# State-space stage: the imaginary input sum of the scan moves from VectorE to GpSimd

## The chip, the cores and the metric

The kernel runs on one core of a Trainium2 chip. The metric is the device time of one execution in microseconds; the time before is the median of three executions. TensorE is called PE, VectorE DVE, ScalarE ACT, GpSimd Pool, and SyncE SP. SP here only issues DMAs.

## The reference, cut to what matters

One decoder layer is applied to 2048 prompt positions and to 64 sample positions: an RMS norm, a diagonal complex state-space mixer (S5), a residual sum, a second norm, a top-2 mixture of 16 experts, and a final norm. The change touches the recurrence of the mixer alone:

```python
lb_re = mag * jnp.cos(ang)
lb_im = mag * jnp.sin(ang)
...
_, _, st_re, st_im = lax.associative_scan(
    _linear_recurrence_combine, (a_re, a_im, bu_re, bu_im), axis=1)
y = (jnp.einsum('gcp,bsgp->bsgc', c_re.astype(f32), st_re)
     - jnp.einsum('gcp,bsgp->bsgc', c_im.astype(f32), st_im)
     + d.astype(f32) * u)
y = jax.nn.gelu(y.reshape(nb, ns, SSM_WIDTH)).astype(x.dtype)
a = y @ w_out
```

There are 32 groups of 64 complex states. The state follows s[k] = lambda * s[k-1] + b[k] with complex lambda. The kernel turns the input back by the angle of lambda to the power k, so that what is left is a real recurrence with the magnitude alone, on the real and on the imaginary part separately; it scans both, and turns the result forward again.

## The kernel before, in words

The kernel has three stages on PE. Stage A projects x to u (until 118 us). Stage B is the state-space stage (118 to 190 us). Stage C is the output projection, gate, norm and router (190 to some 440 us), and after it come the expert matmuls, bound by PE, until the end.

Stage B works in `PR` = 16 rounds r, each for two of the 32 groups, on 128 partitions (2 groups x 64 states) by 256 chunks of 8 positions. `turns(r)` gives the cosine and sine tables of the round in `WT`. For each round:

- PE `b_state(r)` (L1196): eight matmuls write the real and imaginary inputs into two PSUM banks (`v_done`).
- DVE `b_rot(r)` (L1767, L1768): `r1` = v x cosine and `r2` = v x sine, both 128x512 (real and imaginary half), v in PSUM and the table in SBUF (`rot_done`). `r1` has two buffers, `r2` has one.
- DVE `b_mix(r)`: `z[:,0]` = r1 real + r2 imaginary (L1782) and `z[:,1]` = r1 imaginary - r2 real (L1785), 128x256 each, all of it in SBUF (`z_done`). `z` has one buffer for both halves.
- DVE `b_scan(r)` (L1775): the scan of the real and then of the imaginary half, into `r1` (`scan_done`).
- DVE `b_turn(r)` (L1793, L1794): scan result x cosine into `Sc`, x sine into `Ss`, 128x512 each, SBUF only (`turned_on`).
- PE `b_out(r)` (L1214, L1219): the direct term from the table `T`, and the states times C, into PSUM (`y_done`). ACT `b_gelu(r)` (L823) writes the result over `U` (`gelu_done`). Pool `b_final(r)` (L524, L525) takes the last state of the round out of `Sc` and `Ss`: two instructions on one column.

DVE issues them in the order rot(r+1), scan(r), mix(r+1), turn(r). Every engine runs its own list in order; semaphores tie them.

The table `T` is filled in four parts n of eight groups each. Pool clears a part (L515 for the first, L529 for the other three, at the head of its rounds 0, 1 and 2) and signals `t_zero`. SP waits for it (L349) and issues eight DMAs from `Kp` into the part (L352); `b_out` waits for a part at rounds 0, 4, 8 and 12. Behind the 32 DMAs of `T`, SP's list goes on with the 4 MB load of `w_out` (L356), the load of the last gain (L358), and then, three times, a store of eight groups of y to DRAM (`y_by_block`, L362, after 8, 16 and 24 GELUs), a wait until it has landed (L363), and eight loads that bring it back in another layout (L365). Stores and loads of the last eight groups follow (L372, L377). Stage C begins on PE with `c_half` (L1259), which waits for all 24 loads of L365 (`y_in`).

Two memsets at Pool's start (L471, L472) have the semaphore `c_pool`, for which ACT (L780) and PE (L1167) wait; ten index tables that Pool makes behind stage B have `consts`, for which DVE waits (L1913).

Of the kernel before, what the change touches and what calls it, by code (L numbers as in the profile page):

```python
# [9 lines left out]
ALU = mybir.AluOpType  # L10
# [14 lines left out]
PR = G // 2  # L25
# [7 lines left out]
EPS = 1e-6  # L33
# [38 lines left out]
def hybrid_kernel(nc, x_rows, x_first, x_cols, s0, par, bc_in, d_in, gmix, gffn, gfin, w_in, w_out, w_route,  # L72
# [9 lines left out]
    with outer:  # L82
        scope = [outer]

        def sb(name, shape, dt=F32):
            return scope[0].enter_context(nc.sbuf_tensor(name, shape, dt))

        def sem(name):
            return outer.enter_context(nc.semaphore(name))
# [8 lines left out]
        ones = sb("ones", [P, P])  # L98
# [38 lines left out]
        epsc = sb("epsc", [P, 1])  # L137
# [23 lines left out]
        r1 = [sb(f"r1{b}", [P, 2, NP_CH]) for b in range(2)]  # L161
        r2 = sb("r2", [P, 2, NP_CH])
        z = sb("z", [P, 2, NP_CH])
# [29 lines left out]
        for n in (0, 1):  # L193
# [65 lines left out]
        wst.close()  # L259


        names = """par_in gm_in bc_in win0 win1 win2 win3 win4 win5 win6 win7 rt_in gl_in dch act_small c_g1 c_pool 
            x_in0 x_in1 xrow_in0 xrow_in1 w1_hi w1_lo xh_done xl_done sq_done std_done rin_done um_done us_done us8_in tr_done ue_act ue_dve
            kd_ready f0_ready ph_ready pws_ready pool_chain cl_ready e_ready wt_small tabs_ready k_done k_evac k_full et_done et_evac
            t_zero t_in0 t_in1 t_in2 t_in3 v_done rot_done z_done scan_done turned_on sp_zero sp_head cl_neg fo_done y_done gelu_done
            y_stored yt_st0 yt_st1 yt_st2 yt_st3 y_in y_tail fo_raw fo_sum st_stored
            wout_in w2_hi w2_lo ys_hi ys_lo a_done sig_done x2_done xr_in0 xr_in1 x2_st0 x2_st1 wr_scaled xt_done xt_evac lt_done lt_evac fold_set rl_done rl_evac ssq_done half_ss dchc
            dchd exp_d consts tab_set tab_clear d_ready pos_done pos_read idx_done tab_early tab_in tab_first tab_ready tot_done words_set words_done ctl_done exp_in rec_set
# [2 lines left out]
        S = {n: sem(n) for n in names}  # L271
# [193 lines left out]
        def _(pool):  # L465
# [2 lines left out]
            ch(pool.affine_select(out=ident[:, :], in_=ident[:, :], compare_op=ALU.not_equal, fill=1.0, base=0,  # L468
                                  pattern=[[-1, P]], channel_multiplier=1))
            ch(pool.memset(power[:, :], -0.5))  # L470
            pool.memset(epsc[:, :], EPS).then_inc(S["c_pool"], 1)  # L471
            pool.memset(ones[:, :], 1.0).then_inc(S["c_pool"], 1)  # L472
            ch(pool.memset(upper[:, :], 1.0))

            ch(pool.affine_select(out=upper[:, :], in_=upper[:, :], compare_op=ALU.is_gt, fill=0.0, base=0,
# [44 lines left out]
            def b_final(r):  # L520

                b = r % SB
                pool.wait_ge(S["turned_on"], 2 * r + 2)
                pool.tensor_tensor(FO[:, 0, r, DECB:DECB + 1], Sc[b][:, 0, NCH:NCH + 1], Ss[b][:, 1, NCH:NCH + 1], ALU.subtract).then_inc(S["fo_done"], 1)  # L524
                pool.tensor_tensor(FO[:, 1, r, DECB:DECB + 1], Sc[b][:, 1, NCH:NCH + 1], Ss[b][:, 0, NCH:NCH + 1], ALU.add).then_inc(S["fo_done"], 1)  # L525

            for r in range(PR):
                if r < 3:
                    pool.memset(T[:, 8 * r + 8:8 * r + 16, :], 0.0).then_inc(S["t_zero"], 1)  # L529
                b_final(r)  # L530
# [175 lines left out]
        def _(act):  # L706
# [70 lines left out]
            act.wait_ge(S["c_g1"], 1)  # L777
            act.activation(AN[:, 3, :, :], AN[:, 1, :, :], ACT.Sin).then_inc(S["act_small"], 1)
            act.activation(AN[:, 4, :, :], AN[:, 2, :, :], ACT.Sin).then_inc(S["act_small"], 1)
            act.wait_ge(S["c_pool"], 2)  # L780
            for t in range(1, TA):
                if t < TA - 1:
                    x_hi(t + 1)
# [305 lines left out]
        def _(pe):  # L1089
            def a_first():  # L1090

                pe.wait_ge(S["xl_done"], 1)
                for k in range(KD):
                    pe.wait_ge(S[f"win{k}"], 16)
                    for h in range(2):
                        mm = pe.matmul(pbig[h * ST:(h + 1) * ST, 0, 0:W // 2], x0g[:, k, :], w1[:, k, h * W // 2:(h + 1) * W // 2],
                                       start=(k == 0), stop=(k == KD - 1))
                mm.then_inc(S["um_done"], 1)
# [65 lines left out]
                        mm = pe.transpose(bank[:, (2 * a + r) * P:(2 * a + r + 1) * P], E[:, a, 2 * f + r, :], ident[:, :])  # L1164
                mm.then_inc(S["et_done"], 1)

            pe.wait_ge(S["c_pool"], 2)  # L1167
            a_first()
            for t in range(1, TA):
                a_tile(t)  # L1170
# [386 lines left out]
        def _(dve):  # L1557
            ch = Chain(dve, S["dch"])
            tt, ts, stt = dve.tensor_tensor, dve.tensor_scalar, dve.scalar_tensor_tensor
# [197 lines left out]
            def turns(r):  # L1757
                return [WT[:, a:a + 1, r, :].to_broadcast([P, 2, NP_CH]) for a in range(2)]

            def b_rot(r):  # L1760

                b = r % 2
                v = pbig[:, 2 * b:2 * b + 2, DECB:NCH]
                dve.wait_ge(S["v_done"], r + 1)
                if r >= 1:
                    dve.wait_ge(S["z_done"], 2 * r)
                tt(r1[b][:, :, :], v, turns(r)[0], ALU.mult).then_inc(S["rot_done"], 1)  # L1767
                tt(r2[:, :, :], v, turns(r)[1], ALU.mult).then_inc(S["rot_done"], 1)  # L1768

            def b_scan(r):  # L1770
                b = r % 2
                dve.wait_ge(S["z_done"], 2 * r + 2)
                mg = mag8[:, r:r + 1].to_broadcast([P, NP_CH])
                for a in range(2):
                    dve.tensor_tensor_scan(r1[b][:, a, :], mg, z[:, a, :], 0.0, ALU.mult, ALU.add).then_inc(S["scan_done"], 1)  # L1775

            def b_mix(r):
                b = r % 2
                dve.wait_ge(S["rot_done"], 2 * r + 2)
                if r >= 1:  # L1780
                    dve.wait_ge(S["scan_done"], 2 * r - 1)
                tt(z[:, 0, :], r1[b][:, 0, :], r2[:, 1, :], ALU.add).then_inc(S["z_done"], 1)  # L1782
                if r >= 1:
                    dve.wait_ge(S["scan_done"], 2 * r)
                tt(z[:, 1, :], r1[b][:, 1, :], r2[:, 0, :], ALU.subtract).then_inc(S["z_done"], 1)  # L1785

            def b_turn(r):
                b, q = r % 2, r % SB
# [5 lines left out]
                tt(Ss[q][:, :, DECB + 1:NCH + 1], r1[b][:, :, :], turns(r)[1], ALU.mult).then_inc(S["turned_on"], 1)  # L1794

            b_rot(0)
            b_mix(0)
            for r in range(PR):
                if r + 1 < PR:
                    if r >= 1:  # L1800
                        dve.wait_ge(S["turned_on"], 2 * r)
                    b_rot(r + 1)
                b_scan(r)
                if r + 1 < PR:
                    b_mix(r + 1)
                b_turn(r)
# [103 lines left out]
                    yy = y_  # L1910

            dch = Chain(dve, S["dchd"])
            dve.wait_ge(S["consts"], 10)  # L1913
            dch(dve.memset(logit[LAST:P, 0, :], 0.0))
            dch(dve.memset(EP[:, 0, :], 0.0))
            dch(dve.memset(te[:, 0, :], 1.0))
# [358 lines left out]
```

## Time and profile before

| | us |
|---|---|
| median of three executions | 825.34 (823.92 to 826.82) |
| profiled execution, whole | 825.51 |
| its span | 823.8 |
| PE busy in the span | 786.2 (95%) |
| DVE busy | 598.0 (73%) |
| ACT busy | 412.6 (50%) |
| Pool busy | 321.7 (39%) |

All times in the text are microseconds from the start of the span. The profiled execution lies 0.17 us above the median and 1.7 us above its own span. The granted clock is a share of 2.4 GHz: 1.00 is that, 0.50 is 1.2 GHz. In a timeline, instructions of one kind that follow each other may stand in one row with a count.

### The profile page before, as it was taken

The page shows a single profiled execution, that of the slowest core. Times are in us where ns is not written, and L with a number is a line of the kernel's source. Part 1 is how long each engine was busy: PE and PEld are TensorE (multiplying, and loading weights), DVE is VectorE, ACT ScalarE, POOL GpSimd, SP SyncE. Part 2 cuts the span into 40 slices and gives each one's busy share as a digit, 9 for nine tenths or more (in the row PEclk, how much of TensorE's full clock was granted, in tenths as well). Part 3 has the DMA queues.
Part 4 walks back from the last instruction along what each step waited for, and adds up shares of the span by engine and source line. Part 5 has one row for each costly group of instructions (what it writes and reads, how often), then busy time and mean ns, then how long its engine had stood idle before and what let it go on. Part 6 is the DMA issues. An engine that isn't in the chain of part 4 may idle for free.

```text
span 823.8 us, 15189 instructions
## 1 busy us (share of the span) xinstructions
PE 786.2 (95%) x4265; PEld 620.0 (75%) x4265; DVE 598.0 (73%) x1143; ACT 412.6 (50%) x770; POOL 321.7 (39%) x416
## 2 busy tenths in 40 slices
PE   6999989999999999999989989999999999999993
PEld 4888866655778787877767878888888888888772
DVE  7997789996533374556876788768687688687843
ACT  7556752124334543333353666657466576466631
POOL 3920011002000001322455576667666766566533
PEclk9999999999999999999999999999999999999997
DMA  8564315989742433424357587658775688786632
GB/s 304 162 225 180 129 25 162 234 165 204 289 154 90 141 121 110 154 78 155 104 214 284 207 306 271 212 180 263 272 256 199 207 291 299 249 301 196 236 121 81
DMA packets 57671, 161.27 MB, mean 196 GB/s; under 512 B 21857, under 2 KB 26465, under 8 KB 50913
## 3 DMA queue, kind: packets, MB, share of 16 engines
q1 hardware_dynamic: 34304, 112.99, 42.0%
q0 software_dynamic: 22976, 47.05, 16.4%
q8 instruction: 44, 0.72, 0.3%
q14 instruction: 59, 0.48, 0.2%
q10 hardware_dynamic: 288, 0.03, 0.0%
HBM read 129.07 MB, written 62.40 MB: 232 GB/s over the span
## 4 chain that ended last, share of the span: by engine, by line
PE 42%; DVE 3%; issue 3%; DVEq 1%; ACT 1%; ACTq 0%; POOL 0%; POOLq 0%
PE pbig L1395 8%; PE pbig L1399 8%; PE pbig L1396 8%; PE pbig L1414 4%; PE pbig L1416 4%; PE pbig L1415 4%; PE pbig L1331 4%; PE pbig L1407 1%; DVE WL L2018 0%; ACT WH L932 0%; DVEq L2128 0%; DVE hh L1863 0%; PE pbig L1352 0%; DVEq L2126 0%; PE pbig L1358 0%
## 5 line engine op out<-in xcount | busy, mean ns | idle before, releaser
L1395 PE MATMUL pbig<-WH,xgH 128*128 (+1 forms) x304 | 123.0, 404 | 1.2 <-issue 1.1
L1396 PE MATMUL pbig<-WL,xgH 128*128 (+1 forms) x304 | 119.0, 391 | 0.0
L553 POOL DMA_INDIRECT records<-rec,at_rec x34 | 38.8, 1140 | 191.2 <-DVEq L2011 158.9
L1278 PE MATMUL pbig<-w2H,ysH 128*128 128x512 f32 x256 | 105.3, 411 | 0.0
L1279 PE MATMUL pbig<-w2L,ysH 128*128 128x512 f32 x256 | 100.6, 393 | 0.0
L1280 PE MATMUL pbig<-w2H,ysL 128*128 128x512 f32 x256 | 100.5, 393 | 0.0
L2018 DVE SCALAR_TENSOR_TENSOR WL<-WR,gf_p,WH 128x512 f32 (+1 forms) x128 | 86.2, 746 | 0.0
L932 ACT ACTIVATE WH<-WR,gf_p 128x512 f32 (+1 forms) x128 | 80.8, 713 | 3.0 <-DMA WR<-in_w_gu 0.9
L1399 PE MATMUL pbig<-WH,xgL 128*128 (+1 forms) x304 | 77.0, 395 | 0.0
L627 POOL DMA_INDIRECT x_sums<-xg,recs x36 | 60.7, 1685 | 35.4 <-DVE xg L2122 21.5
L2122 DVE SCALAR_TENSOR_TENSOR xg<-pbig,recs,xg 128x1024 f32<-128x1024 f32 x39 | 49.9, 1280 | 27.8 <-PE pbig L1416 27.8
L950 ACT ACTIVATE sl<-pbig,recs 128x256 f32<-128x256 f32 x40 | 19.0, 475 | 98.0 <-PE pbig L1399 92.6
L1395 PEld LDWEIGHTS pbig<-WH,xgH 128*128 128x128 f32 x304 | 57.1, 188 | 14.4 <-issue 2.5
L1399 PEld LDWEIGHTS pbig<-WH,xgL 128*128 128x128 f32 x304 | 57.0, 188 | 13.7
L1414 PE MATMUL pbig<-WH,hTH 128*128 (+1 forms) x160 | 66.4, 415 | 0.0
L1396 PEld LDWEIGHTS pbig<-WL,xgH 128*128 128x128 f32 x304 | 57.1, 188 | 11.3
L1890 DVE TENSOR_TENSOR x<-pbig,sg 128x1024 f32<-128x1024 f32 x16 | 19.6, 1223 | 62.8 <-PE pbig L1280 58.3
L1416 PE MATMUL pbig<-WH,hTL 128*128 (+1 forms) x160 | 63.3, 396 | 0.0
L1415 PE MATMUL pbig<-WL,hTH 128*128 (+1 forms) x160 | 62.5, 390 | 0.0
L1278 PEld LDWEIGHTS pbig<-w2H,ysH 128*128 128x128 f32 x256 | 48.2, 188 | 13.8 <-issue 4.6
L1863 DVE SCALAR_TENSOR_TENSOR hh<-pbig,recs,sl 128x256 f32<-128x256 f32 x40 | 19.3, 483 | 53.4 <-issue 28.8
L655 POOL DMA_INDIRECT out_y<-fo,recs x40 | 49.6, 1240 | 19.2 <-issue 9.9
(356 smaller groups left out, 1745.9 us busy)
## 6 DMA issues: line engine op xcount, KB each, us to landing
WR<-in_w_gu SPq DMA_DIRECT2D x32, 1024.0 KB
WR<-in_w_dn SPq DMA_DIRECT2D x16, 1024.0 KB
xT<-in_x_cols SPq DMA_DIRECT2D x16, 512.0 KB, 3.6
low<-in_x_rows SPq DMA_DIRECT2D x16, 512.0 KB, 4.3
U<-in_x_rows SPq DMA_DIRECT2D x16, 512.0 KB, 5.4
x_mid<-x SPq DMA_DIRECT2D x16, 512.0 KB
x_sums<-x SPq DMA_DIRECT2D x16, 512.0 KB
w<-in_w_out SPq DMA_DIRECT2D x1, 4096.0 KB, 13.7
```

Of the source, the lines that this page charges most:

```text
L627: pool.indirect_dma_start(sumD, bass.IndirectOffsetOnAxis(ap=recs_u[:, t, SUM_AT:SUM_AT + 1], axis=0), xg[t % RING][:, :], None, bounds_ch ...
L932: act.activation(WH[:, ds(to + k * 2 * DE, 2 * DE)], WR[:, k * 2 * DE:(k + 1) * 2 * DE], ACT.Copy, scale=gf_p[:, k:k + 1]).then_inc(S["hi_ ...
L1278: pe.matmul(pbig[:, n, :], ysH[b][:, k, :], w2H[n][:, k, :], start=(k == 0), stop=False)
L1279: pe.matmul(pbig[:, n, :], ysH[b][:, k, :], w2L[n][:, k, :], start=False, stop=False)
L1280: mm = pe.matmul(pbig[:, n, :], ysL[b][:, k, :], w2H[n][:, k, :], start=False, stop=(k == CB - 1))
L1395: pe.matmul(pbig[:, 6, :], xgH[b][:, k, :], WH[:, ds(off + k * 2 * DE, 2 * DE)], start=(k == 0), stop=False)
L1396: pe.matmul(pbig[:, 6, :], xgH[b][:, k, :], WL[:, ds(low_ + k * 2 * DE, 2 * DE)], start=False, stop=False)
L1399: mm = pe.matmul(pbig[:, 6, :], xgL[b][:, k, :], WH[:, ds(off + k * 2 * DE, 2 * DE)], start=False, stop=(k == KD - 1))
L1414: pe.matmul(out, hTH[b][:, k, :], WH[:, w], start=(k == 0), stop=False)
L1415: pe.matmul(out, hTH[b][:, k, :], WL[:, ds(low_ + at, 512)], start=False, stop=False)
L1416: mm = pe.matmul(out, hTL[b][:, k, :], WH[:, w], start=False, stop=(k == 1))
L2018: stt(WL[:, ds(low_ + w, 2 * DE)], WR[:, w:w + 2 * DE], gf_p[:, k:k + 1], WH[:, ds(to + w, 2 * DE)].bitcast(F32), ALU.mult, ALU.subtract). ...
```

## The change

The instruction L1785 leaves `b_mix` on DVE. Pool gets a function `b_mix_im(r)`, which computes the same subtraction after `rot_done` of round r and after both scans of round r-1. Pool issues it for round 0 ahead of its round loop, and for round r+1 at the head of iteration r, ahead of the memset of `T` and of `b_final(r)`. It signals a new semaphore `z_im`. On DVE, `b_rot(r)` waits for `z_done` r and for `z_im` r; `b_scan` waits for `z_done` ahead of the real scan and for `z_im` ahead of the imaginary one. The semaphore `c_pool` is merged into `consts`, whose last wait becomes 12.

```diff
-            pool.memset(epsc[:, :], EPS).then_inc(S["c_pool"], 1)
-            pool.memset(ones[:, :], 1.0).then_inc(S["c_pool"], 1)
+            pool.memset(epsc[:, :], EPS).then_inc(S["consts"], 1)
+            pool.memset(ones[:, :], 1.0).then_inc(S["consts"], 1)
...
+            def b_mix_im(r):
+
+                b = r % 2
+                pool.wait_ge(S["rot_done"], 2 * r + 2)
+                if r >= 1:
+                    pool.wait_ge(S["scan_done"], 2 * r)
+                pool.tensor_tensor(z[:, 1, :], r1[b][:, 1, :], r2[:, 0, :], ALU.subtract).then_inc(S["z_im"], 1)
+
+            b_mix_im(0)
             for r in range(PR):
+                if r + 1 < PR:
+                    b_mix_im(r + 1)
                 if r < 3:
                     pool.memset(T[:, 8 * r + 8:8 * r + 16, :], 0.0).then_inc(S["t_zero"], 1)
                 b_final(r)
...
                 if r >= 1:
-                    dve.wait_ge(S["z_done"], 2 * r)
+                    dve.wait_ge(S["z_done"], r)
+                    dve.wait_ge(S["z_im"], r)
                 tt(r1[b][:, :, :], v, turns(r)[0], ALU.mult).then_inc(S["rot_done"], 1)
                 tt(r2[:, :, :], v, turns(r)[1], ALU.mult).then_inc(S["rot_done"], 1)

             def b_scan(r):
                 b = r % 2
-                dve.wait_ge(S["z_done"], 2 * r + 2)
                 mg = mag8[:, r:r + 1].to_broadcast([P, NP_CH])
                 for a in range(2):
+                    dve.wait_ge(S["z_im" if a else "z_done"], r + 1)
                     dve.tensor_tensor_scan(r1[b][:, a, :], mg, z[:, a, :], 0.0, ALU.mult, ALU.add).then_inc(S["scan_done"], 1)
...
                 tt(z[:, 0, :], r1[b][:, 0, :], r2[:, 1, :], ALU.add).then_inc(S["z_done"], 1)
-                if r >= 1:
-                    dve.wait_ge(S["scan_done"], 2 * r)
-                tt(z[:, 1, :], r1[b][:, 1, :], r2[:, 0, :], ALU.subtract).then_inc(S["z_done"], 1)
...
-            dve.wait_ge(S["consts"], 10)
+            dve.wait_ge(S["consts"], 2 + 10)
```

The waits of ACT and PE for `c_pool` 2 become waits for `consts` 2.

## Rows read from the trace of the kernel before

**Rows 1.** Timeline of PE, stage B (start, us, engine, line, operation, [idle before <- releaser]).
```profile
126.23 1.11 PE L1196 MATMUL pbig<-U,E 128*64 128x264 f32 x8
...
130.34 1.11 PE L1196 MATMUL pbig<-U,E 128*64 128x264 f32 x8
...
188.97 0.61 PE L1219 MATMUL pbig<-turned_s,CLn 64*128 64x264 f32 x4
190.63 5.37 PE L1259 MATMUL pbig<-w,U 128*64 128x512 f32 x24 [1.05 <-DMA U<-y_by_block]
```

**Rows 2.** Timeline of SP's DMA queue, stage B (when SP issued; not the landing).
```profile
114.84 21.52 SPq L352 DMA_DIRECT2D T<-Kp  x32
136.40 0.59 SPq L356 DMA_DIRECT2D w<-in_w_out  x1
...
139.36 0.33 SPq L362 DMA_DIRECT2D y_by_block<-U  x1
154.38 3.65 SPq L365 DMA_DIRECT2D U<-y_by_block  x8
158.07 0.43 SPq L362 DMA_DIRECT2D y_by_block<-U  x1
167.08 3.62 SPq L365 DMA_DIRECT2D U<-y_by_block  x8
174.16 0.34 SPq L362 DMA_DIRECT2D y_by_block<-U  x1
180.01 3.62 SPq L365 DMA_DIRECT2D U<-y_by_block  x8
```

**Rows 3.** Windows: each engine's busy time, then granted clock, DMA share, GB/s.
```profile
168.00:176.00 8.00, 7.65 (x52) 4.63 (x50) 7.97 (x16) 1.71 (x8) 0.33 (x2) 1.00 1.13 143
```

**Rows 4.** Timeline of DVE: one large product, the head of stage B, and round 0.
```profile
111.49 1.22 DVE L1709 TENSOR_TENSOR WT<-WT,tabs 128x1024 f32<-128x1024 f32 x1
...
118.80 0.43 DVE L1782 TENSOR_TENSOR z<-r 128x256 f32<-128x256 f32 x1
...
119.66 0.69 DVE L1767 TENSOR_TENSOR r<-pbig,WT 128x512 f32<-128x512 f32 x1
...
120.87 1.26 DVE L1775 TENSOR_TENSOR_SCAN r<-sm,z 128x256 f32<-128x256 f32 x2
122.05 0.40 DVE L1782 TENSOR_TENSOR z<-r 128x256 f32<-128x256 f32 x1
122.36 0.42 DVE L1785 TENSOR_TENSOR z<-r 128x256 f32<-128x256 f32 x1
122.70 0.69 DVE L1793 TENSOR_TENSOR turned_c<-r,WT 128x512 f32<-128x512 f32 x1
...
124.02 0.69 DVE L1767 TENSOR_TENSOR r<-pbig,WT 128x512 f32<-128x512 f32 x1
```

**Rows 5.** Timeline of Pool: a 256-element product, a memset, a one-element sum.
```profile
35.94 1.62 POOL L488 TENSOR_TENSOR low<-WT,tabs 128x256 f32<-128x256 f32 x1
...
114.92 0.95 POOL L529 MEMSET T<- 128x1024 f32 x1
...
185.09 0.51 POOL L524 TENSOR_TENSOR FO<-turned_c,turned_s 128x1 f32<-128x1 f32 x1 [4.03 <-DVE turned_s L1794]
```

**Rows 6.** Timeline of DVE beside the Pool product of rows 5.
```profile
35.26 1.82 DVE L1668 TENSOR_TENSOR p<-tabs 128x1152 f32<-128x1152 f32 x1
37.00 1.77 DVE L1669 TENSOR_TENSOR CL<-tabs 128x1152 f32<-128x1152 f32 x1
38.81 1.66 DVE L1670 TENSOR_TENSOR CL<-p,CL 128x1152 f32<-128x1152 f32 x1
```

**Rows 7.** Windows as in rows 3: early in stage A, and behind PE's last matmul.
```profile
50.00:52.00 2.00, 2.00 (x7) 1.54 (x6) 1.97 (x2) 0.63 (x3) 0.00 (x0) 0.50 0.91 356
...
810.00:811.00 1.00, 0.39 (x2) 0.00 (x0) 0.57 (x1) 0.81 (x3) 0.70 (x2) 1.00 0.44 176
...
813.00:814.00 1.00, 0.00 (x0) 0.00 (x0) 0.59 (x1) 0.00 (x0) 0.81 (x2) 0.66 0.00 0
```

More of the change, by code:

```diff
@@ L259, in hybrid_kernel @@
         wst.close()
-        names = """par_in gm_in bc_in win0 win1 win2 win3 win4 win5 win6 win7 rt_in gl_in dch act_small c_g1 c_pool
+        names = """par_in gm_in bc_in win0 win1 win2 win3 win4 win5 win6 win7 rt_in gl_in dch act_small c_g1
             x_in0 x_in1 xrow_in0 xrow_in1 w1_hi w1_lo xh_done xl_done sq_done std_done rin_done um_done us_done us8_in tr_done ue_act ue_dve
             kd_ready f0_ready ph_ready pws_ready pool_chain cl_ready e_ready wt_small tabs_ready k_done k_evac k_full et_done et_evac
-            t_zero t_in0 t_in1 t_in2 t_in3 v_done rot_done z_done scan_done turned_on sp_zero sp_head cl_neg fo_done y_done gelu_done
+            t_zero t_in0 t_in1 t_in2 t_in3 v_done rot_done z_done z_im scan_done turned_on sp_zero sp_head cl_neg fo_done y_done gelu_done
             y_stored yt_st0 yt_st1 yt_st2 yt_st3 y_in y_tail fo_raw fo_sum st_stored
@@ L779, in _ @@
             act.activation(AN[:, 4, :, :], AN[:, 2, :, :], ACT.Sin).then_inc(S["act_small"], 1)
-            act.wait_ge(S["c_pool"], 2)
+            act.wait_ge(S["consts"], 2)
             for t in range(1, TA):
@@ L1165, in e_spread @@
                 mm.then_inc(S["et_done"], 1)
-            pe.wait_ge(S["c_pool"], 2)
+            pe.wait_ge(S["consts"], 2)
             a_first()
```

## The prediction

> **What bounds the kernel now.** The page says that PE is busy for 95% of the span, so time is lost or won where PE waits. I read PE's timeline first, around the edited stage. In stage B a round of PE, from one `b_state` to the next, takes 4.11 us while nothing holds it [rows 1]: its own work. DVE's timeline has no idle time in stage B; its round takes 4.36 us, from L1767 at 119.66 to L1767 at 124.02 [rows 4], so DVE paces the stage from about round 5 on and shortening its list looks like a gain. But PE's last matmul of stage B ends at 189.58 (188.97 + 0.61), and the first matmul of stage C starts at 190.63, with 1.05 us idle put down to the DMA that brings y back [rows 1]. What releases stage C is not DVE's last round. It is the chain on SP's queue.
>
> So the third view is SP's timeline [rows 2]. Thirty-two DMAs of `T` are issued in one run from 114.84, then `w_out` at 136.40, the first store of y at 139.36. SP's next instruction, the loads, starts at 154.38, when that store has landed. Loads, store 2 at 158.07, landed at 167.08; loads, store 3 at 174.16, landed at 180.01; loads, and 190.63 is 10.6 behind them. Is that chain bound by the GELUs or by the transfers? Store 2 was issued right behind its loads and landed 12.70 after store 1. Store 3 was issued 3.39 later than it could have been (174.16 against 170.77, which is 167.08 + the 3.69 that SP needed the time before), since it waited for 24 GELUs; it landed 12.93 after store 2. **Issuing it 3.39 us late cost 0.23.** The transfers bound the chain: the loads in small pieces keep the DMA engines full (share 1.13) from 168 to 176 at only 143 GB/s [rows 3], and the store queues behind them.
>
> Two consequences. A faster DVE gives at most 0.23 us back. And whatever delays the landing of store 1 reaches stage C nearly in full.
>
> **The change part by part.**
>
> *Semaphore `c_pool` merged into `consts`*: the same number of signals and waits. The first two signals still come first, as Pool's list has them at its start. Nothing.
>
> *L1785 leaves DVE.* Its slot is 122.36 to 122.70 [rows 4], so 0.34 a round is saved.
>
> *Pool makes the difference while DVE works.* The Pool instruction for round r+1 may start when both scans of round r are done. Behind them DVE has L1782, L1793 and L1794, all with two inputs from SBUF. How the two engines go beside each other is in the early part of the trace: Pool's 256-element product takes 1.62 (35.94 to 37.56) [rows 5] while DVE's product of 1152 elements ends at 37.08 (35.26 + 1.82) [rows 6]. Pool is done 0.48 after DVE's instruction ends; it has waited for it. DVE pays too: alone a 1024-element product takes 1.22 and a 256-element one 0.40 [rows 4], which is 0.82 for 768 elements, so 1152 elements take 1.22 + 128 x 0.82/768 = 1.36 alone, but the three took 1.82, 1.77 and 1.66 [rows 6]: 0.46, 0.41 and 0.30 more, in the mean 0.39. The scan does it as well: the one-element sum of Pool that lay beside a scan took 0.51 [rows 5]. So the handover works at the ends of instructions, and I price it at 0.39 on DVE for each Pool instruction, with 0.30 and 0.46 as ends. The net on a round is 0.39 - 0.34 = +0.05, between -0.04 and +0.12.
>
> The Trainium skill, page "SBUF — State Buffer", section "Who interferes with whom", says that a VectorE instruction with two SBUF inputs and a GpSimd instruction that reads SBUF exclude each other, and that whoever starts first holds the port for the whole instruction. The waiting in rows 5 and 6 agrees. By the page "GPSIMD Engine Reference" a two-input operation needs at least some 2.5 cycles per element, an estimated 0.53 us here; by both rules DVE would lose 0.53 a round, +0.19 net, which would leave my sum as it is, since the sum doesn't go by the round.
>
> *New waits on DVE.* `b_rot(r+2)` now waits for Pool's result. Pool is ready at L1782's end + 0.48. In round 0 that is 122.45 + 0.48 = 122.93, against 124.02 for L1767: 1.1 us of cover. If Pool lost each handover until L1794 had ended, it would be done 0.48 behind it, and a round would be 0.48 + 0.07 - 0.34 = +0.19 to +0.25 longer. The wait ahead of the second scan is met long before. At the very start there is no cover: L1782 ends at 119.23, Pool at 119.71, and with 0.07 of handing on (an estimate from the gap between dependent Pool instructions such as L488 and the next) the second L1767 starts at 119.78 instead of 119.66: +0.12, once. Over 16 rounds DVE is late by 0.12 + 16 x 0.05 = 0.9 us (-0.5 to +2.0). PE's stage B then ends at 190.5.
>
> *The memset of `T` moves behind two of the new instructions.* This is the step that decides. Before, Pool cleared part 1 at 114.92, long before SP wanted it [rows 5]. Now that memset stands behind `b_mix_im(0)` and `b_mix_im(1)`, and the latter needs both scans of round 0. These end at 120.87 + 1.26 = 122.13, plus 0.12: 122.25. L1782 then holds Pool until 122.57, Pool ends at 123.05, the memset (0.95) at 124.0, SP sees it at 124.1. SP wants it after its first eight DMAs: 114.84 + 8 x 21.52/32 = 120.22 [rows 2]. **SP stands still for 3.9 us.** Ends: 3.4 if Pool's instruction took some 0.2 and never waited, 4.6 if it also waited for L1793. The memsets of parts 2 and 3 come at some 128.4 and 132.8 and SP wants them at 129.5 and 134.9: no more loss. No `b_out` suffers: round 1 needs its part at 126.23 + 1.04 [rows 1], so round 4 needs part 1 three PE rounds later, at 139.6, and its last DMA is issued by 129.5.
>
> Behind the `T` DMAs everything on SP is 3.9 later: `w_out` at 140.3. Store 1 waits behind it, at 141.4 instead of 139.36. It landed 18.0 us behind the issue of `w_out` (136.40 to 154.38) [rows 2], with 4 MB ahead of it on the same queue. I take that distance as fixed: store 1 lands at 158.3, +3.9. Bounds: +2.0 if only its own issue counted, +4.6 with the worst memset. Store 2 lands at 158.3 + 12.70 = 171.0, SP is free for store 3 at 174.7; its GELUs are ready at 174.16 + 0.12 + 12 x 0.05 = 174.9. As 3.4 us of lateness cost 0.2, this 0.2 costs nothing, and it lands 12.7 to 12.9 later, at 183.7. Against 180.01 that is +3.7: the 3.9 less the 0.2 that the idle time gives back. Only if the round of DVE grew by more than 0.3 (3.7 over 12 rounds) would the GELUs come last.
>
> *Stage C* starts at 190.63 + 3.7 = 194.3. ACT makes its first copy of y, the last GELUs and the weight copies behind the same loads, and the last stores and loads follow in SP's list, so all of these move with it. Behind 190.63 PE is nearly always busy and the rest hangs on it; I see nothing that would take the 3.7 back.
>
> **Sum.** 825.51 + 3.7 = 829.2 for an execution like the profiled one, which was 0.17 above the median; against 825.34 it is 829.0, +0.45%.
>
> **Rivals.**
>
> *A. The transfers take the delay back, and it is not slower.* Store 1 may not have been bound by the bytes of `w_out` but by its own issue; then it lands 2.0 later, store 3 1.8 later, and the time is 827.1, within 0.3%. For it: the DMA engines were not full in every slice between 136 and 154. Against it: 15 us for 1 MB where store 3 took 5.9. It decides from a landing of store 1 before 157.1 (+2.7) on. 15%.
>
> *B. PE's clock falls in the longer gap.* PE would stand still from 190.5 to 194.3. Behind its last matmul, which ends inside 810 to 811, the granted clock is down to 0.66 in 813 to 814 [rows 7]; this gap would be as long. Elsewhere the clock stood at 0.50 (1.2 GHz) for a whole stretch of 2 us [rows 7]; 2 to 3.4 us like that at the head of stage C would cost 1.0 to 1.7: 830.5. Against it: the gap may be a little too short. 11%.
>
> *C. The port costs more than the early rows say, and DVE's round becomes the bound.* From +0.3 a round on each further 0.1 costs 1.6 us at the end of stage B; +0.5 gives 197.6 for PE's end, +7: 832.4. Against it: three rows with at most 0.46 of loss, and even when Pool loses all handovers the round grows by only 0.25. 6%.
>
> *D. The gain that the edit seems to promise.* With a free port DVE's round would be 4.02 and PE's 4.11 would pace; 0.25 us saved in each of some ten rounds. But stage C would still wait for the loads, at best at 190.4, and the memset slips all the same. Faster by over 0.3% would need the `T` DMAs not to slip. 2%.
>
> **How the numbers follow.** The forecast, +3.2 to +4.5 with 3.7 as its middle, has 66%; A 15%, B 11%, C 6%, D 2%. One measurement tells about 0.3% (2.5 us) from no change. Slower: 66 + 11 + 6 = 83%, less 1 for forecasts that end short: 82%. Same: 16%. Faster: 2%. The range goes down to 827.0, to take in most of A, and up to 831.2, for B and the upper end of the slip.
>
> **What would show it.** In the trace after: SP waits some 3.9 us at L349 for Pool's memset of `T`, in the middle of the `T` DMAs; `w_out` is issued near 140.3; the three y stores land near 158.3, 171.0 and 183.7; the first L1259 starts near 194.3 behind some 3.8 us of idle, put down to the DMA. DVE's L1793 takes some 1.05 instead of 0.69, its round 4.3 to 4.5; Pool's new instruction shows about 0.7 to 0.8. I am wrong in the DMA step if `w_out` is late and L1259 is not, and in the port step if the round is below 4.2 or above 4.6.

## The result and the profile after

| | before | after |
|---|---|---|
| median, us | 826.07 (823.92 to 829.35, 5 executions) | 835.12 (830.19 to 838.24, 5 executions) |
| profiled execution, whole | 825.51 | 830.19 |
| its span | 823.8 | 828.4 |

The change makes the kernel slower: ratio 1.0101, 95% interval 1.0067 to 1.0134. That is 9 us between the medians, where 3.7 were forecast and the range ended at 831.2. (The ratio is an estimate of its own, not the quotient of the two medians; the same holds for the runs below.) The profiled execution is the fastest of the five of the changed kernel, and it is only 4.7 above the profiled one of before. So two things need an explanation: the 4.7, and why the other executions are longer still.

Line numbers of the kernel after are higher: L1767/L1768 are now L1779/L1780, L1782 is L1794, L1775 is L1787, L1793/L1794 are L1802/L1803, PE's L1259 is L1270; Pool's new instruction is L533 and its memset L540. SP's lines are unchanged.

The timeline of SP's DMA queue after, which answers to [rows 2]:

```profile
113.35 26.16 SPq L352 DMA_DIRECT2D T<-Kp  x32
139.55 0.59 SPq L356 DMA_DIRECT2D w<-in_w_out  x1
...
140.65 0.43 SPq L362 DMA_DIRECT2D y_by_block<-U  x1
158.79 3.64 SPq L365 DMA_DIRECT2D U<-y_by_block  x8
162.48 0.43 SPq L362 DMA_DIRECT2D y_by_block<-U  x1
172.15 3.62 SPq L365 DMA_DIRECT2D U<-y_by_block  x8
175.81 0.44 SPq L362 DMA_DIRECT2D y_by_block<-U  x1
184.47 3.62 SPq L365 DMA_DIRECT2D U<-y_by_block  x8
```

The run of `T` DMAs lasts 26.16 instead of 21.52. Everything behind it is late by that, and by some more.

Pool after, the head of stage B, which answers to [rows 5]:

```profile
117.35 0.96 POOL L533 TENSOR_TENSOR z<-r 128x256 f32<-128x256 f32 x1 [3.85 <-DVE r L1780]
121.42 0.76 POOL L533 TENSOR_TENSOR z<-r 128x256 f32<-128x256 f32 x1 [3.11 <-DVE r L1787]
122.12 0.95 POOL L540 MEMSET T<- 128x1024 f32 x1
```

SP would have wanted part 1 at 113.35 + 5.4 = 118.7. The memset that clears it ends at 123.07 (122.12 + 0.95), 4.3 later.

DVE after, which answers to [rows 4]:

```profile
117.31 0.42 DVE L1794 TENSOR_TENSOR z<-r 128x256 f32<-128x256 f32 x1
118.81 0.69 DVE L1779 TENSOR_TENSOR r<-pbig,WT 128x512 f32<-128x512 f32 x1 [1.08 <-POOL z L533]
...
121.20 0.40 DVE L1794 TENSOR_TENSOR z<-r 128x256 f32<-128x256 f32 x1
121.51 1.21 DVE L1802 TENSOR_TENSOR turned_c<-r,WT 128x512 f32<-128x512 f32 x1
122.65 0.68 DVE L1803 TENSOR_TENSOR turned_s<-r,WT 128x512 f32<-128x512 f32 x1
123.36 0.69 DVE L1779 TENSOR_TENSOR r<-pbig,WT 128x512 f32<-128x512 f32 x1
```

L1802 takes 1.21 where L1793 took 0.69; the round is 4.55 (118.81 to 123.36) instead of 4.36. And PE where stage B ends, which answers to [rows 1]:

```profile
191.04 0.61 PE L1230 MATMUL pbig<-turned_s,CLn 64*128 64x264 f32 x4
195.11 6.74 PE L1270 MATMUL pbig<-w,U 128*64 128x512 f32 x24 [3.45 <-DMA U<-y_by_block]
```

PE is done with stage B at 191.65 (191.04 + 0.61) and stands still for 3.45 us, released by the DMA. The windows (columns as in [rows 3]) show the clock there:

```profile
190.00:192.00 2.00, 1.65 (x16) 1.09 (x12) 1.81 (x1) 0.00 (x0) 0.34 (x4) 1.00 1.15 134
192.00:194.00 2.00, 0.00 (x0) 0.00 (x0) 0.49 (x1) 0.00 (x0) 1.93 (x10) 1.00 1.10 162
194.00:196.00 2.00, 0.89 (x3) 0.34 (x5) 0.56 (x2) 1.12 (x4) 1.45 (x1) 0.63 0.51 184
196.00:198.00 2.00, 2.00 (x8) 0.79 (x6) 0.47 (x2) 2.00 (x2) 0.00 (x0) 0.52 0.69 145
198.00:200.00 2.00, 2.00 (x12) 0.67 (x10) 2.00 (x1) 2.00 (x2) 0.00 (x0) 1.00 1.09 235
```

The granted clock falls while PE waits (the window from 194 to 196 has 0.63 in the mean, the next one 0.52, where 0.50 is 1.2 GHz), and stage C's first matmuls run on it. The 24 of them take 6.74 and end at 201.85 (195.11 + 6.74), where they took 5.37 before [rows 1].

One thing disturbs the comparison. Stage B itself starts 1.5 us earlier after (first L1779 at 115.98, first L1767 before at 117.47). That is no gain of the change: in the execution of before the clock stood at 0.50 between 50 and 52 [rows 7], and after it was 1.00 from 48 to 52. So I compare distances from the first L1767 or L1779, called the start of stage B from here on. The third column is a second trace of the changed kernel, from the first experiment.

| us | before | after | after, second trace |
|---|---|---|---|
| run of `T` DMAs | 21.5 | 26.2 | 26.7 |
| `w_out` issued to store 1 landed | 18.0 | 19.2 | 19.3 |
| store 1 landed to store 3 landed | 25.6 | 25.7 | 26.4 |
| store 3 landed to first matmul of stage C | 10.6 | 10.6 | 10.4 |
| start of stage B to first matmul of stage C | 73.2 | 79.1 | 80.3 |
| its 24 matmuls | 5.4 | 6.7 | 7.6 |
| end of these to end of span | 627.8 | 626.6 | 631.8 |

In the first pair of traces: -1.5 from stage A, +6.0 at the start of stage C, +1.4 in its first matmuls, -1.3 behind it (which no row here explains), in all +4.6, the difference of the spans.

### The profile page after: what moved, and what is told of

It reads as the page before. It is cut to its first block, busy times and chain, and to the rows that moved or that the text cites. A ratio compares the mean times of both kernels' runs of the same rounds, so it can differ in the third digit from the quotient of the medians.

```text
span 828.4 us, 15218 instructions
## 1 busy us (share of the span) xinstructions
PE 785.5 (95%) x4265; PEld 618.2 (75%) x4265; DVE 600.5 (72%) x1127; ACT 411.8 (50%) x770; POOL 334.2 (40%) x432
## 4 chain that ended last, share of the span: by engine, by line
PE 38%; DMA 3%; DVE 3%; issue 2%; DVEq 1%; POOL 1%; ACTq 1%; ACT 1%; SPq 0%; POOLq 0%
PE pbig L1406 7%; PE pbig L1410 7%; PE pbig L1407 7%; PE pbig L1425 4%; PE pbig L1427 4%; PE pbig L1426 4%; PE pbig L1342 4%; PE pbig L1418 1%; DMA records<-rec,at_rec 1%; DMA xg<-x_mid,recs 1%; DMA WR<-in_w_gu 1%; DVE WL L2027 1%; POOL records L564 1%; DMA low<-records 1%; ACT WH L943 1%
## 5 line engine op out<-in xcount | busy, mean ns | idle before, releaser
L638 POOL DMA_INDIRECT x_sums<-xg,recs x36 | 63.3, 1758 | 34.9 <-DVE xg L2131 25.5
L1872 DVE SCALAR_TENSOR_TENSOR hh<-pbig,recs,sl 128x256 f32<-128x256 f32 x40 | 19.3, 483 | 52.6 <-ACT sl L961 49.4
L1291 PEld LDWEIGHTS pbig<-w2H,ysL 128*128 128x128 f32 x256 | 48.1, 188 | 11.2
```

What stands on the lines that cost most here:

```text
L638: pool.indirect_dma_start(sumD, bass.IndirectOffsetOnAxis(ap=recs_u[:, t, SUM_AT:SUM_AT + 1], axis=0), xg[t % RING][:, :], None, bounds_ch ...
L1291: mm = pe.matmul(pbig[:, n, :], ysL[b][:, k, :], w2H[n][:, k, :], start=False, stop=(k == CB - 1))
```

## The experiments

Ratios are to the kernel before on the same chip.

**The changed kernel again.** No edit.

> The changed kernel once more, for a second trace and the granted clock of more executions. Chain theory: SP's T DMAs end some 4.6 us later against the first L1779 of DVE than before, the three stores of y land some 5.9 us later, and the first L1270 starts 79.1 us behind the first L1779 (before: 73.2). Clock theory: PE stands still for over 3 us ahead of L1270, the clock goes to 0.50 to 0.63 somewhere in the 4 us behind it, and executions with a lower mean clock are longer. Ratio 1.006 to 1.012. Port rival: the stage would end with PE waiting for DVE's last L1803 and no idle time put down to a DMA.

Median 835.91 (832.51 to 838.77), ratio 1.0099 (1.0066 to 1.0131). The chain came out as expected and a little worse: stage C begins at 80.3. Its trace, 837.0 us long, shows PE's first group of stage C and, in windows, where its clock was low.

```profile
197.54 7.63 PE L1270 MATMUL pbig<-w,U 128*64 128x512 f32 x24 [4.59 <-DMA U<-y_by_block]
...
196.00:200.00 4.00, 2.46 (x6) 0.85 (x8) 0.89 (x2) 2.69 (x4) 0.75 (x1) 0.50 0.59 171
200.00:204.00 4.00, 4.00 (x16) 1.41 (x14) 3.70 (x2) 3.79 (x3) 0.00 (x0) 0.73 1.05 216
492.00:496.00 4.00, 3.53 (x10) 2.79 (x11) 4.00 (x6) 2.25 (x2) 1.88 (x3) 0.57 0.98 362
```

The gap is 4.59 and the matmuls behind it take 7.63. The clock falls once more at 492, behind a short stall of PE in the expert stage: PE is idle there for 2.29, and for 1.5 to 2.6 in the other traces, also in those where the clock doesn't fall (2.22 in the trace of before). The mean granted clock of an execution goes with its time: over the 11 executions of the changed kernel it is 0.984 to 0.992, median 0.986; over 32 executions of before, 0.984 to 0.994, median 0.990.

**The memsets put first.** GpSimd keeps its subtractions; only the order on Pool changes.

```diff
+            for r in range(3):
+                pool.memset(T[:, 8 * r + 8:8 * r + 16, :], 0.0).then_inc(S["t_zero"], 1)
             b_mix_im(0)
             for r in range(PR):
                 if r + 1 < PR:
                     b_mix_im(r + 1)
-                if r < 3:
-                    pool.memset(T[:, 8 * r + 8:8 * r + 16, :], 0.0).then_inc(S["t_zero"], 1)
                 b_final(r)
```

> The changed kernel with the three later memsets of T put ahead of Pool's first subtraction, so that SP never waits for them; GpSimd keeps its subtractions. Chain theory: T DMAs end 21.5 us after their start as before, the stores land as before (62.5 us behind the first L1779), and the first L1270 follows PE's stage B without a gap, some 75.8 us behind the first L1779 instead of 79.1: 3.3 us won of the change, 4.6 with the clock that no longer falls; still 2.6 us slower than before because DVE's round is 4.55 instead of 4.36. Ratio to before 1.002 to 1.004. Port rival (DVE's round is what costs): no change against the changed kernel, 1.007 to 1.010.

Median 828.31, ratio 1.0019 (0.9997 to 1.0042). Most of the loss is gone. SP and PE:

```profile
114.96 22.23 SPq L352 DMA_DIRECT2D T<-Kp  x32
...
193.20 5.37 PE L1270 MATMUL pbig<-w,U 128*64 128x512 f32 x24
```

The `T` run is 22.23; L1270 follows stage B without idle time, 75.6 behind the start of stage B, and takes 5.37. What remains is DVE's lateness: it starts its second L1779 0.64 late and each of 15 rounds takes 0.19 more, 3.5 in all. PE's stage B ends at 75.6 instead of 72.1; stage C began at 73.2 before, because it waited for the loads, so 2.4 of the 3.5 are felt.

**The memsets late, in the kernel before.** Nothing is on GpSimd that wasn't before; each memset waits for the scans.

```diff
                 if r < 3:
+                    pool.wait_ge(S["scan_done"], 2 * r + 2)
                     pool.memset(T[:, 8 * r + 8:8 * r + 16, :], 0.0).then_inc(S["t_zero"], 1)
```

> The kernel before, with nothing moved to GpSimd, but with each of the three later memsets of T waiting for both scans of its round. Chain theory: SP stands still for some 3 us, w_out goes out 3 us later, the stores land 3 to 4.3 later, L1259 starts 3 to 4.3 later (76.2 to 77.5 us behind the first L1767), with PE's stage B ended at 72.1: a gap of over 4 us, so the clock falls at the head of stage C and costs 1.3 more. Ratio 1.004 to 1.008. Port rival: the time of before within 0.2%, as DVE's round stays 4.36.

Median 833.49, ratio 1.0075 (1.0049 to 1.0101). This is the other half, and the stronger one:

```profile
113.89 24.91 SPq L352 DMA_DIRECT2D T<-Kp  x32
...
194.96 6.87 PE L1260 MATMUL pbig<-w,U 128*64 128x512 f32 x24 [6.34 <-DMA U<-y_by_block]
```

DVE's round is untouched, and PE waits 6.34 us for the loads, with the clock down behind it. Stage C begins at 78.4 (194.96 less 116.53), 0.9 later than the end of what I expected. So the late memsets alone cost 0.75%, **about three quarters of the 0.99% to 1.01% that the change costs**, and the work on GpSimd alone 0.19%, which the interval doesn't tell from nothing. The two costs don't simply add: in the changed kernel PE ends stage B at 75.7 (191.65 less 115.98) and then waits for the loads, so that DVE's lateness doesn't reach stage C. What GpSimd's subtractions add there is a later memset: the run of `T` DMAs is 26.2 to 26.7 long, and 24.9 here.

**PE kept busy in the gap.**

```diff
             pe.wait_ge(S["fo_raw"], PR)
+            pe.wait_ge(S["wout_in"], 16)
+            for i in range(6):
+                pe.matmul(pbig[:, 0, :], ident[:, :], w2[:, 0, 0:512], start=True, stop=True)
```

> The changed kernel with six extra matmuls of 512 columns in PE's gap ahead of L1270; their results are not used. Clock theory: the clock stays at 1.00 behind the gap, the 24 matmuls of L1270 take 5.4 us instead of 6.7, and the kernel is 1.3 us faster than the changed one, or up to 1.7 where the fall was a full one. Chain theory: L1270 starts where it did. If the lower clock of the slower executions is made elsewhere, these executions stay as slow as those of the changed kernel.

Median 834.03, ratio 1.0089 (1.0061 to 1.0118): 1.9 us less than the changed kernel beside it, though the two intervals overlap, so it is the trace that shows the effect. PE and the clock:

```profile
191.66 5.42 PE L1259 MATMUL pbig<-w,ident 128*128 128x512 f32 x12
197.01 5.37 PE L1273 MATMUL pbig<-w,U 128*64 128x512 f32 x24
...
192.00:196.00 4.00, 4.00 (x10) 1.71 (x9) 0.56 (x1) 0.00 (x0) 3.46 (x11) 1.00 1.08 191
196.00:200.00 4.00, 4.00 (x17) 1.25 (x17) 1.87 (x3) 3.96 (x5) 0.00 (x0) 1.00 0.63 124
```

The clock stays at 1.00 and the 24 matmuls are back at 5.37. The extra ones took 5.4, more than the gap, so part of the win is given back: stage C begins 81.0 behind the start of stage B. The mean clocks of the six executions are 0.990 to 0.992, so the low ones of the changed kernel came from this place in the main.

**The same with three.** `range(3)` in place of `range(6)`.

> As the run with six extra matmuls, but three (12 rows of the trace became 6, 2.7 us), which end ahead of y's landing. Clock theory: the gap is down to 1 us or so, L1270 starts where it does in the changed kernel (79 to 80.3 us behind the first L1779), its 24 matmuls take 5.4, and the median falls below the 834.0 of the six, to 831 to 833, with mean clocks of 0.990 to 0.992. If the clock at the gap didn't matter the median stays at 835 to 836.

Median 833.47, ratio 1.0093 (1.0071 to 1.0116); stage C begins at 79.4 (196.75 less 117.38):

```profile
196.75 5.37 PE L1273 MATMUL pbig<-w,U 128*64 128x512 f32 x24 [0.94 <-issue]
```

The median is 0.6 below that of the six, but they ran on two chips, and against the kernel before on its own chip the ratio isn't lower; it is also above the 831 to 833 that I expected. The clocks are 0.988 to 0.992, and the trace has a fall at 488 to 496. So the times don't tell three from six. In the matmuls themselves the fall at the gap costs 1.4 to 2.3 (6.74 and 7.63 against 5.37), some 2 us of the 9 to 10.

**w_out ahead of part 2 of T, in the changed kernel.** The memsets stay late.

```diff
             for n in range(G // 8):
                 sp.wait_ge(S["t_zero"], n + 1)
+                if n == 2:
+                    sp.wait_ge(S["tr_done"], FILLS)
+                    sp.dma_start(w2[:, :, :], w_out).then_inc(S["wout_in"], 16)
...
-            sp.wait_ge(S["tr_done"], FILLS)
-            sp.dma_start(w2[:, :, :], w_out).then_inc(S["wout_in"], 16)
...
             def second_turn(n):
...
-                if n == 1:
+                if n == 2:
                     pe.wait_ge(S["pos_read"], len(BATCHES))
```

The last hunk takes a wait out of PE's list in a later stage; it can't touch what is read here, the start of stage C. The ratio includes it; in the kernel before, with and without it, the ratios don't differ beyond their intervals (the next two runs).

> The changed kernel, its late memsets included, with one move on SP: the 4 MB load of w_out goes out ahead of part 2 of the T DMAs instead of behind part 3, so that store 1 doesn't queue behind it. Chain theory: the T DMAs still end some 4.6 us late, but store 1 lands within 7 us of its issue, store 3 leaves as soon as its 24 GELUs are there, and L1270 starts right behind PE's stage B, 75.7 us behind the first L1779 instead of 79 to 80; no gap, no fall of the clock there. Ratio to before 1.002 to 1.004, as with the memsets put first. If the late T DMAs themselves cost, or the DVE round alone, it stays at 1.008 to 1.010.

Median 827.84, ratio 1.0022 (1.0000 to 1.0044). The rows are:

```profile
114.80 16.06 SPq L355 DMA_DIRECT2D T<-Kp  x16
130.96 0.53 SPq L352 DMA_DIRECT2D w<-in_w_out  x1
131.53 16.74 SPq L355 DMA_DIRECT2D T<-Kp  x16
...
193.03 5.37 PE L1271 MATMUL pbig<-w,U 128*64 128x512 f32 x24
```

Stage C's matmuls (L1271 here) follow stage B without a gap at 75.6 (193.03, start of stage B at 117.43), as with the memsets first. The last `T` DMA goes out 33.5 behind the first (148.27 less 114.80), far later than the 4.6 that I had expected, and still nothing is lost at the start of stage C. So late `T` DMAs cost nothing there by themselves; in the changed kernel they cost because 4 MB and the first store of y stand behind them.

**The same move in the kernel before**, both hunks.

> The same move on SP in the kernel before. Chain theory: stage C no longer waits for the loads; L1259 starts at the end of PE's stage B, 72.1 us behind the first L1767 instead of 73.2, and the kernel is 1.0 us faster than before, 0.9985 to 0.9995, which can hardly be told from no change by time. Rival: w_out beside the T DMAs delays a T part and PE waits in round 8 or 12; then slower.

Median 825.58, ratio 0.9993 (0.9975 to 1.0012). Stage C begins at 72.0 (189.44 less 117.42). No `T` part is missed. And **without the hunk in `second_turn`**, which makes it the clean one:

> The kernel before with nothing but the load of w_out moved ahead of part 2 of the T DMAs (the wait at PE's second turn is as before). L1259 starts at the end of PE's stage B, 72.0 behind the first L1767 instead of 73.2; 1.1 us faster, 0.9980 to 0.9995, within what can be told from no change.

Median 824.97, ratio 0.9985 (0.9960 to 1.0010); stage C again at 72.0. The trace shows the 1.1 us, the times can't tell it from no change.

**Half on each engine**, with the memsets first: Pool makes 128 of the 256 columns.

```diff
-                pool.tensor_tensor(z[:, 1, :], r1[b][:, 1, :], r2[:, 0, :], ALU.subtract).then_inc(S["z_im"], 1)
+                pool.tensor_tensor(z[:, 1, 0:HALF], r1[b][:, 1, 0:HALF], r2[:, 0, 0:HALF], ALU.subtract).then_inc(S["z_im"], 1)
...
                 tt(z[:, 0, :], r1[b][:, 0, :], r2[:, 1, :], ALU.add).then_inc(S["z_done"], 1)
+                if r >= 1:
+                    dve.wait_ge(S["scan_done"], 2 * r)
+                tt(z[:, 1, HALF:NP_CH], r1[b][:, 1, HALF:NP_CH], r2[:, 0, HALF:NP_CH], ALU.subtract).then_inc(S["z_done"], 1)
```

> The changed kernel with the memsets first, and each engine making half (128 columns) of the imaginary sum. Port theory, price by element: with 256 columns L1802 took 1.21 instead of 0.69, 0.52 for 256; with 128 it takes 0.95, and the DVE round is 4.55 - 0.26 + 0.20 = 4.49. If the price is mostly fixed, L1802 stays at 1.1 to 1.2 and the round is 4.70. Time within 0.2% of the kernel with the memsets first in both cases.

Median 824.95, ratio 0.9998 (0.9976 to 1.0021). DVE's timeline:

```profile
120.31 0.40 DVE L1796 TENSOR_TENSOR z<-r 128x256 f32<-128x256 f32 x1
120.63 0.55 DVE L1799 TENSOR_TENSOR z<-r 128x128 f32<-128x128 f32 x1
121.10 0.68 DVE L1807 TENSOR_TENSOR turned_c<-r,WT 128x512 f32<-128x512 f32 x1
```

Here it is the half instruction that waits (0.55), not L1807: whichever DVE instruction is the second behind the scan pays. The round is 4.49 as expected (117.93 to 122.42), which makes the price 4.49 - (4.36 - 0.34 + 0.20) = 0.27 for 128 columns, half of the 0.53 for 256. The 0.20 for DVE's own half instruction alone is an estimate, half of what the whole one takes; no row shows it undisturbed. Pool's rows say the same without it: its half instruction ends 0.31 behind L1796 (120.54 + 0.48 against 120.31 + 0.40), the whole one 0.58 behind L1794 (121.42 + 0.76 against 121.20 + 0.40 in the changed kernel), so that 128 columns make 0.27. The price goes by the elements.

**One operand repeated**, with the memsets first. Only what Pool reads as its second operand changes.

```diff
-                pool.tensor_tensor(z[:, 1, :], r1[b][:, 1, :], r2[:, 0, :], ALU.subtract).then_inc(S["z_im"], 1)
+                pool.tensor_tensor(z[:, 1, :], r1[b][:, 1, :], r2[:, 0, 0:1].to_broadcast([P, NP_CH]), ALU.subtract).then_inc(S["z_im"], 1)
```

> The changed kernel with the memsets first; Pool's second operand is one column of r2 repeated 256 times instead of 256 columns, so the imaginary sum is not the reference's: only the trace is of interest. If the price on DVE is set by the operand elements that Pool reads through the port, L1802 falls from 1.21 to 0.95 to 1.05, as with the products of stage A whose second operand is repeated too (0.30 to 0.46). If it is set by the number of output elements, L1802 stays at 1.21.

The two engines:

```profile
122.51 0.64 POOL L533 TENSOR_TENSOR z<-r 128x256 f32<-128x256 f32 x1 [3.11 <-DVE r L1787]
...
122.59 1.10 DVE L1802 TENSOR_TENSOR turned_c<-r,WT 128x512 f32<-128x512 f32 x1
```

The median is 826.11, ratio 1.0001 (0.9964 to 1.0038). L1802 takes 1.10, between the two expectations, and the round is 4.44. A repeated operand is cheaper on Pool and on DVE by 0.11 each, so the operand reads count, but not alone. Pool's products in stage A, from which I had taken my price, are of this kind: they read a table repeated 16 times, and cost DVE 0.39 in the mean [rows 6]; this one costs 0.42.

**Pool beside the rotation.** A second buffer for `r2`, and Pool's instruction for round r+1 held until the turn of round r has ended, so that it lies beside L1779 and L1780, which read only one input from SBUF. The memsets are first.

```diff
-        r2 = sb("r2", [P, 2, NP_CH])
+        r2 = [sb("r2", [P, 2, NP_CH]), low[:, D:D + 2 * NP_CH].rearrange("p (a k) -> p a k", a=2)]
...
-                    pool.wait_ge(S["scan_done"], 2 * r)
+                    pool.wait_ge(S["turned_on"], 2 * r)
...
-                if r >= 1:
-                    dve.wait_ge(S["z_done"], r)
-                    dve.wait_ge(S["z_im"], r)
+                if r >= 2:
+                    dve.wait_ge(S["z_done"], r - 1)
+                    dve.wait_ge(S["z_im"], r - 1)
```

> The changed kernel with the memsets first, a second buffer for r2, and Pool's subtraction of round r+1 held until L1803 of round r has ended, so that it runs beside DVE's L1779 and L1780, which read one of their inputs from PSUM. Port theory: Pool takes no time from DVE there, L1802 is back at 0.69 and DVE's round falls to 4.02 to 4.11, where PE paces. Chain theory: w_out still goes ahead of store 1, so this whole gain is worth at most 0.2 us: PE's stage B ends some 69 us behind the first L1779 instead of 72.1, and L1270 still starts at 73.0 to 73.8, now behind a gap of some 4 us, with the clock down behind it; ratio 1.000 to 1.004. If DVE's round were what counts: 0.995.

Median 831.45, ratio 1.0052 (1.0031 to 1.0073). DVE and PE:

```profile
120.82 0.69 DVE L1802 TENSOR_TENSOR turned_c<-r,WT 128x512 f32<-128x512 f32 x1
...
191.76 6.78 PE L1270 MATMUL pbig<-w,U 128*64 128x512 f32 x24 [6.89 <-DMA U<-y_by_block]
```

L1802 is back at 0.69: beside the rotation the port costs DVE nothing. PE ends stage B at 184.86, 68.4 behind its start, against 72.1 before. And the kernel is **slower than before**, though DVE and PE are faster in stage B: stage C still waits for the loads and begins at 75.3, behind a gap of 6.89 us with the clock down. This is what the forecast said of rival D, and worse. The 75.3 is above the 73.0 to 73.8 expected, and the ratio above the 1.000 to 1.004: `w_out` to store 1 takes 19.1 here, and store 1 to store 3 26.4, both longer than in the trace of before. Why they are longer no run shows.

**Pool beside the rotation and w_out early.** Both edits together, the second without the hunk in `second_turn`.

> The same with w_out ahead of part 2 of the T DMAs, so that neither the port nor the queue is in the way. PE paces stage B at 4.11 a round, 24 GELUs are there some 54 us behind the first L1779, store 3 lands 4 to 5 later and L1270 starts 10.6 behind that, at 69 to 70 instead of 73.2 before: 3 to 4 us faster than before, ratio 0.9945 to 0.997. If it is above 0.998 one of the two causes is not what I take it for.

Median 821.08 (818.54 to 823.31), ratio 0.9940 (0.9916 to 0.9965): **faster than both kernels**. SP, PE, and a round of DVE with Pool's instruction beside it:

```profile
171.14 0.34 SPq L363 DMA_DIRECT2D y_by_block<-U  x1
176.10 3.62 SPq L366 DMA_DIRECT2D U<-y_by_block  x8
...
186.76 7.07 PE L1271 MATMUL pbig<-w,U 128*64 128x512 f32 x24 [1.99 <-DMA U<-y_by_block]
...
142.81 0.73 POOL L534 TENSOR_TENSOR z<-r 128x256 f32<-128x256 f32 x1 [3.10 <-DVE turned_s L1804]
...
142.78 0.69 DVE L1780 TENSOR_TENSOR r<-pbig,WT 128x512 f32<-128x512 f32 x1
...
146.89 0.69 DVE L1780 TENSOR_TENSOR r<-pbig,WT 128x512 f32<-128x512 f32 x1
```

The round is 4.11, PE's own. Store 3 leaves when its GELUs are there and lands 5.0 later; stage C begins 70.4 behind the start of stage B (116.38), 2.8 earlier than before and a little above the 69 to 70 expected; PE is done with stage B at 68.4, and waits for the loads. Even here PE idles 1.99 and the first 24 matmuls take 7.07, with the clock at 0.50 until past 190. With `w_out` alone, in the kernel before, the median was 824.97 and the ratio 0.9985. The rest, 3.9 between the medians, comes from what this run has besides: the subtraction on GpSimd beside the rotation, the memsets first, and the second buffer for `r2`. What each gives alone wasn't run.

## Why the prediction was right and where it failed

The sum was +3.7, all of it at the start of stage C, and the median came out 9 higher. The steps that failed are three terms of that sum: SP's stop and the fixed distance behind it were too small (stage C begins 5.9 and 7.1 later, not 3.7), and what the clock costs in the longer gap was left out, as a rival with 11%, where it cost 1.4 and 2.3. Some 1 to 2 us of the loss are not explained. That the profiled execution came within 1.0 of the 829.2 forecast for it is luck: of the 7.4 that were lost in the trace at the start of stage C and in its first matmuls, 1.5 in stage A and 1.3 behind these matmuls were made good, and neither was forecast.

**Right: what bounds the start of stage C, and the step that decides.** The view of SP's queue named it: the first matmul of stage C is released by the loads, and the memset behind `b_mix_im(1)` delays them. The late memsets alone gave 1.0075, and moving `w_out` out of the way undid most of the loss (1.0022) without touching the memsets. That a faster DVE alone gives nothing back was shown by the run with Pool beside the rotation.

**Mis-sized: the stop of SP.** Forecast 3.9, measured 4.6 and 5.2 (26.16 and 26.74 less 21.52). The memset itself ends 4.3 behind the time at which SP wanted its part; the rest, 0.3 and 0.9, is about what the run of `T` DMAs differs by where no memset is late (21.5 to 22.2). The step that failed is the handing over from Pool at the head: I gave the second L1767 a delay of 0.12. It starts 1.50 behind L1794 where it started 0.86 behind L1782, which is 0.64 late. Pool's first subtraction ended 0.58 behind the end of L1794 (118.31 against 117.73), not 0.48, and DVE went on 0.50 after Pool's shown end, not 0.07. Scans, second subtraction and memset all inherit that. The 0.96 of the first subtraction is no cost of its own: the next one takes 0.76, but started later beside its L1794, and also ends 0.58 behind it. What makes the 0.50 stays open; with 128 columns DVE went on at most 0.24 after Pool's shown end (117.69 to 117.93).

**Wrong: the distance from `w_out` to the landing of store 3, taken as fixed.** I carried 18.0 + 25.6 = 43.6 over from the one trace of before. After, it is 44.9 and 45.7, and with late memsets in the kernel before 45.8. A possible reason, not shown, is that store 1 is now issued 1.1 us behind `w_out` and not 3.0, and stores 2 and 3 follow their loads at once, so that nothing in the queue runs ahead. The distance from `w_out` to store 1 points that way (17.9 to 19.1 in the four runs with the memsets first, 19.2 to 19.4 in the five traces with late ones), but the two groups all but touch, and within the first the distance doesn't follow the time at which store 1 was issued: 18.7 with memsets first and 17.9 with one operand repeated, where it was issued 3.6 behind `w_out` in both. I have not tested it by itself.

**Wrong: the chance of rival B.** I gave 11% to the clock falling in the gap, and left its cost out of the sum. It fell to 0.50 in each of the four traces with a longer gap (3.45, 4.59, 6.34 and 6.89), and even with 1.99; with 1.05, in the kernel before, it didn't. Behind the four the 24 matmuls took 1.4 to 2.3 us longer, where I had written 1.0 to 1.7. My gap was 3.7 us, and the row behind PE's last matmul [rows 7] was the evidence; the reason against it had no row at all.

**Wrong: the price of the port, though it hardly enters.** Forecast 0.39 on DVE for each Pool instruction, measured 0.53; round 4.55, not 4.41. The row that I took was of another kind of product: one operand was repeated. The rules of the Trainium skill that I had set beside it (page "GPSIMD Engine Reference", section "2.1 Instruction dispatch": some 2.5 cycles per element with two inputs; page "SBUF — State Buffer", section "Who interferes with whom": the two instructions exclude each other) gave an estimated 0.53. The trace agrees: 4.55 less 4.02 is 0.53. At either price DVE's lateness didn't reach stage C while the loads were later; with the memsets first it is all that remains, 2.4 us at the start of stage C.

**Not in the forecast: how far executions of one kernel differ.** The sum was made for one execution, and for that pair it is 4.7 against 3.7. But the clock fell at 48 to 52 in the execution of before and not in that of after, which hides 1.5; and in eight of the twelve other traces it also falls somewhere between 480 and 496. Median against median the change costs 9 to 10: some 6 to 7 at the start of stage C, some 2 for the clock behind the gap. The rest, some 1 to 2 us, I can't place: the fall near 490 is there in the second trace of the changed kernel and not in the first, and it is there in runs without a gap too, as with the memsets first. What decides whether it comes stays open.

Rivals A, C and D did not come about: store 1 landed late, DVE's round grew by 0.19 and not by the 0.3 from which C counts, and the kernel got slower.

## What to carry to other kernels

Before moving an instruction to another engine, write down what stands behind it in that engine's list and who waits for that: here three late memsets of 0.95 us, wanted by the DMA queue, cost 0.75% by themselves, and the arithmetic by itself 0.19%. Where an engine is done with its own work and waits for a DMA, if only for 1 us, it isn't the bound; look for what is queued ahead of that DMA, and take large loads out of its way before speeding up anything else. And where work goes to GpSimd, choose what VectorE does beside it: the same instruction cost VectorE 0.53 us beside products of two SBUF inputs and nothing beside products with one in PSUM.

## What the runs showed of the hardware

- A GpSimd subtraction of two 128x256 inputs delays a VectorE instruction with two SBUF inputs by 0.53 us, one of 128 columns by 0.27, and one with a repeated operand by 0.42; beside a VectorE instruction with one input in PSUM it takes 0.73 us and delays nothing.
- A GpSimd subtraction that met a VectorE instruction with two SBUF inputs ended 0.58 us behind it (128x256) or 0.31 us behind it (128x128). VectorE, waiting for the first one, went on 0.50 us after its shown end.
- A GpSimd memset beside such a VectorE instruction delayed nothing: L1803 took 0.68 us beside the memset from 122.12 to 123.07.
- With PE idle for 3.45, 4.59, 6.34 and 6.89 us the granted clock fell to 0.50, and the 24 matmuls behind took 6.7 to 7.6 us instead of 5.4; behind 1.99 us idle in one trace it fell too (7.07 us). The mean granted clock of executions of one kernel ranged from 0.984 to 0.994, and their times by 11 us.
- A 1 MB store of y behind a 4 MB and a 0.5 MB load (`w_out` and the gain) landed 17.9 to 19.4 us behind the issue of the first; with the 4 MB load ahead of part 2 of the `T` DMAs it landed 6.6 us after its own issue (148.95 to 155.54 in the changed kernel).
